# Attention tiles of a head pair ordered by query block first and head second, with the two heads' value products interleaved

## The reference

```python
sc = jnp.einsum('bhsd,bhmd->bhsm', q, mk).astype(jnp.float32) * (q.shape[-1] ** -0.5)
p = jax.nn.softmax(sc, axis=-1)
return jnp.einsum('bhsm,bhmd->bhsd', p.astype(mv.dtype), mv)
```

## Time and profile before

| what | value |
|---|---|
| median of 3 runs | 3445.1 us (3441.52 to 3446.01) |
| the profiled execution, its time | 3441.26 us |
| its span, first to last instruction | 3439.4 us |
| mean granted TensorE clock | 0.960 |
| PE busy | 3222.5 us, 94% of the span |
| DVE / ACT / POOL busy | 1401.9 / 745.3 / 1974.3 us |

### The profile page before, as it was taken

The page is one execution under the profiler, slowest core; times in us unless marked ns, Lnnn a source line. Parts: engine busy times, 40 slices in busy tenths (PEclk is TensorE's granted clock), DMA queues, the critical chain, the costliest instruction groups (busy, mean ns, idle before and its releaser), DMA issues.

```text
span 3439.4 us, 44451 instructions
## 1 busy us (share of the span) xinstructions
PE 3222.5 (94%) x14188; PEld 2516.5 (73%) x14188; DVE 1401.9 (41%) x2310; ACT 745.3 (22%) x1516; POOL 1974.3 (57%) x1528
## 2 busy tenths in 40 slices
PE   5898999999979889999999879989999999999998
PEld 3654887888756468788887656868888777878886
DVE  5545225221355352353425545452214544452223
ACT  3421102100234211120102335241002333230001
POOL 5234666776743266677767131847768433747765
PEclk8897999999989899999999889999999999999999
DMA  4111223222221122222222010322223111312222
GB/s 151 37 50 56 98 93 106 94 98 98 92 92 45 35 87 93 100 87 97 98 98 100 28 68 13 118 69 98 97 94 110 62 50 50 110 64 97 98 98 86
DMA packets 78347, 284.97 MB, mean 83 GB/s; under 512 B 8688, under 2 KB 9200, under 8 KB 77424
## 3 DMA queue, kind: packets, MB, share of 16 engines
q1 hardware_dynamic: 74736, 269.41, 23.1%
q10 hardware_dynamic: 3456, 13.50, 1.1%
HBM read 280.78 MB, written 2.10 MB: 82 GB/s over the span
## 4 chain that ended last, share of the span: by engine, by line
PE 78%; DVE 9%; ACT 3%; issue 1%; DVEq 0%; DMA 0%; ACTq 0%
PE pd L512 35%; PE pa L512 34%; PE pd L656 3%; PE po L675 3%; PE pa L664 1%; DVE b_lo L180 1%; DVE work L180 1%; DVE work L184 1%; ACT work L176 1%; DVE h_lo L188 1%; PE pd L575 1%; DVE pair L180 1%; DVE t L188 1%; PE pd L693 1%; PE po L707 1%
## 5 line engine op out<-in xcount | busy, mean ns | idle before, releaser
L465 POOL TENSOR_SCALAR w_hi<-w_raw 128x1024 fp32r<-128x1024 f32 x508 | 550.2, 1083 | 1392.9 <-PE pa L512 884.4
L512 PE MATMUL pa<-h_hi,w_hi 128*128 128x512 f32 x1888 | 754.1, 399 | 24.7 <-DVE h_lo L188 16.9
L469 POOL TENSOR_TENSOR w_lo<-w_raw,w_hi 128x512 fp32r<-128x512 f32 x508 | 743.5, 1464 | 0.0
L512 PE MATMUL pa<-h_lo,w_hi 128*128 128x512 f32 x1888 | 739.5, 392 | 0.0
L512 PE MATMUL pa<-h_hi,w_lo 128*128 128x512 f32 x1888 | 739.3, 392 | 0.0
L467 POOL TENSOR_TENSOR w_lo<-w_raw,w_hi 128x512 fp32r<-128x512 f32 x508 | 703.2, 1384 | 42.3
L512 PE MATMUL pd<-b_hi,w_hi 128*128 128x512 f32 x1152 | 456.8, 397 | 24.4 <-DVE b_lo L180 21.1
L512 PE MATMUL pd<-b_lo,w_hi 128*128 128x512 f32 x1152 | 452.4, 393 | 0.0
L512 PEld LDWEIGHTS pa<-h_hi,w_hi 128*128 128x128 f32 x1888 | 357.3, 189 | 129.8 <-issue 52.8
L512 PE MATMUL pd<-b_hi,w_lo 128*128 128x512 f32 x1152 | 451.7, 392 | 0.0
L512 PEld LDWEIGHTS pa<-h_lo,w_hi 128*128 128x128 f32 x1888 | 357.8, 190 | 75.9 <-issue 3.6
(11 more groups left out here) (154 smaller groups left out, 3417.9 us busy)
## 6 DMA issues: line engine op xcount, KB each, us to landing
w_raw<-in_w SPq DMA_DIRECT2D x508, 512.0 KB, 3.2
mrg<-in_mem ACTq DMA_DIRECT2D x4, 1024.0 KB, 4.8
mrg<-in_nabias ACTq DMA_DIRECT2D x2, 2048.0 KB, 8.7
x_res<-in_x SPq DMA_DIRECT2D x8, 256.0 KB, 5.7
out_y<-mrg ACTq DMA_DIRECT2D x8, 256.0 KB, 2.1
mrg<-in_count ACTq DMA_DIRECT2D x2, 512.0 KB, 3.9
kbuf<-in_delta ACTq DMA_DIRECT2D x2, 448.0 KB, 7.9
rope<-in_rope SPq DMA_DIRECT2D x1, 512.0 KB, 11.8
```

The costliest lines, as they stand in the source:

```text
L465: nc.gpsimd.tensor_scalar(w_hi[:, j], raw[:, j % RR], 1.0, 1.0, ALU.mult, ALU.mult).then_inc(rounded, 1)
L469: nc.gpsimd.tensor_tensor(w_lo[:, j, 512:1024], raw[:, j % RR, 512:1024], w_hi[:, j, 512:1024].bitcast(F32), ALU.subtract).then_inc(wsplit, 1)
L512: ins = mm(out, a, b, start=(first and k == 0 and e == 0), stop=(last and k == k_n - 1 and e == 2))
```

## The change

The list of tiles now has the query block outside and the head inside, so that the two tiles of a step are the two heads of one query block. Their scores are neighbours in PE's stream, from different halves of the rows and into different `pd` banks. The value products are collected until both tiles of the step are there (so both copies of `pt` are waited for ahead of the first product), and then issued alternately, head 0's first key block, head 1's first, head 0's second and so on; each tile's last product signals `pv_done`. For cross, with one head, the order of the products is unchanged, and only the two waits stand ahead of them. All engines follow the new list.

```diff
-        self.tiles = [(j, i) for j in range(self.heads) for i in range(ST)]
+        self.tiles = [(j, i) for i in range(ST) for j in range(self.heads)]
...
-                base = {}
+                base, two = {}, []
...
                         wait_read(pe, n, base[p, a])
-                        for k in range(kn):
-                            kt = NA_TILES[i][k] if ph.kind == "na" else k0 + k
-                            ins = mm(bank[ph.out_rows(j), P * i:P * i + P], ph.values(vbuf, p, j, kt),
-                                     pt[:, g % 2, k * P:k * P + P], start=(k == 0), stop=(k == kn - 1))
-                        ins.then_inc(pv_done, 1)
+                        kts = NA_TILES[i] if ph.kind == "na" else range(k0, k0 + kn)
+                        two.append([(bank[ph.out_rows(j), P * i:P * i + P], ph.values(vbuf, p, j, kt),
+                                     pt[:, g % 2, k * P:k * P + P], k) for k, kt in zip(range(kn), kts)])
+                        if a % 2 == 0:
+                            continue
+                        order = [x for both in zip(*two) for x in both] if ph.heads == 2 else two[0] + two[1]
+                        two.clear()
+                        for dst, val, prob, k in order:
+                            ins = mm(dst, val, prob, start=(k == 0), stop=(k == kn - 1))
+                            if k == kn - 1:
+                                ins.then_inc(pv_done, 1)
```

## The result

The changed kernel took 3423.95 us (median of four runs, 3419.4 to 3431.3) against 3444.55 in the same job (3441.5 to 3446.0): a ratio of 0.9943, interval 0.9922 to 0.9965. It is 20.6 us faster, a third of the 60 us forecast, and 6 us beyond the slow end of the range.

What follows compares the result with a forecast made beforehand. PE's stream was taken as the bound (busy 94%); 26 (dil) + 22 (mem, na) + 9 (swa) + 4 (mla) - 1 (cross) = 60 us gave 3385 us. Range: 8 in 10 between 3364 and 3418.

Steps and rivals of the forecast that it cites:

- drains at each change of the column half: Rival, value products: 0.15 us per change, 49 us, total 3464 or 3494; chance 0.06 together with any other loss.
- no overlap: Rival, scores and products: PE takes heads as it took tiles, only the order acts, 3445 within 3 us; chance 0.08.
- I take 11 us a layer, 22 us: Mem and na of both hybrid layers: 13.8 us a layer saved at full clock, less waits, leaves 22 us.
- It costs under 10 us, within the range: Rival, slow stretches of mem and swa: less busy PE stays at 1.2 GHz longer; under 10 us, no separate chance.
- I deducted 0.9 us where a wait follows directly: Mem and na: savings right before PE's waits for DVE only lengthen the wait, about 0.9 us each.
- dil, "26 us": Dil: 24.5 us for seven pairs with a successor and 1.5 for the last pair, 26 us gained.
- The 3.5 us a pair: Dil: 4.29 us saved of a pair's 31.5, 0.8 given back, 3.5 us gained for each pair with a successor.
- the bank wait: Dil, last step of a pair: the second score waits for the bank the rotation used, 0.8 us given back.
- The last pair ... I give it 1.5: Dil's last pair, without pieces, with DVE and ACT on its path: 1.5 us gained.
- swa, "9 us": Swa: 12 us for four pairs at full clock, three quarters taken because of waits after the rotation: 9 us gained.
- mla, "4 us": Mla: scores can't overlap, products could save 8.7 us, about half hidden by waits for DVE: 4 us gained.
- cross, "1 us lost": Cross: first of the last two tiles' products waits for both copies, about 0.5 us in each of two layers.

Runs made afterwards that it cites:

- early tails: Changed kernel, but in cross and each attention's last four tiles a head's products start with its own copy: 3415.35 us against 3447.06, ratio 0.9901.
- the control: Kernel before the change, with eleven unused matmuls in each na: 3444.83 us against 3445.63, ratio 1.0000.
- fillers are many: Unused matmuls in seven places of mem, na, swa, mla: on top of early tails 3415.46 us, in the kernel before 3450.98, both against 3446.9.
- na's fillers: Early tails plus seven and four unused matmuls in two places of na: 3405.52 us against 3450.12, ratio 0.9870.
- the order-only kernel: Changed kernel with products head by head and an 8-column full-array matmul between a step's two scores: 3475.99 us against 3447.06, ratio 1.0085.

## Why the prediction was wrong

**Right: the overlap and its prices.** Both kinds run two heads in one head's time, 0.63 and 0.59 us a step of two blocks against 0.64 and 0.59 forecast, and a pair of dil takes 28.35 us, inside the 27 to 30 that the prediction set as its test. One of the rivals, drains at each change of the column half, is excluded by the same rows, and "no overlap" too. On the same 128 rows sixteen records of two heads took 1.02 us, and eight of one head alone took 1.02 too. The Trainium skill's rule that a weight load overlaps matmuls in flight only when its row group differs ("TensorE: Matmul & The Clock Gate", Part 3, "The mechanism") does not hold for these products.

**The steps that failed: "I take 11 us a layer, 22 us" for mem and na, and "It costs under 10 us, within the range" for the clock.** Of the 39 us that are missing, the first term is the larger and the better measured: 4.1 us were lost in the windows, and nothing gained in the profile of the version with the products head by head, so about 22 are missing there. The prediction counted every step as work that PE bounds and deducted single waits, but the kernel before has 17.6 us of the second layer's na in its chain without a piece of PE (above).

The clock was named as a rival, placed in mem and swa, and left out of the sum. It fell in both halves of the hybrid layers' attentions, na most (141 to 208 us 0.97 before, 0.88 after), in the retention and pooling behind the second layer by 0.01, and in dil; in swa it is the same within 0.01. The granted clock of whole runs is 0.952 (median after) against 0.957 to 0.959 (medians of before in the later jobs). What a clock step is worth the single runs suggest: the five of the early tails run from 3406.93 us at 0.956 to 3419.89 at 0.951, 2.6 us for each thousandth, those of the control from 3439.38 at 0.961 to 3450.34 at 0.957, 2.7. Five to seven thousandths at 2.6 make 13 to 18 us, an estimate, and not under 10. This is a relation between runs of one kernel and not a measurement of the clock's price; between kernels it fails where fillers are many (0.006 more clock and no time, twice). What shows the cause are the two edits that take it away: early tails (9.9 us of waits, 8.5 us of time) and na's fillers (clock, 6 to 10 us). Together they bring back some 15 to 18 of the 39.

**The rest, term by term** (lengths from the windows, profiled executions, which differ by 10 us and not by 20.6).
- *mem and na, "22 us"*: -4.1, the wrong sign. I deducted 0.9 us where a wait follows directly, but PE saved 0.9 us in every step of a chain whose pace DVE sets at several places, and the wait for both copies (0.40 and 1.03 us) came on top. Then the clock fell from 0.91 to 0.83 and from 0.89 to 0.82.
- *What was not in the sum at all*: the unchanged work behind both attentions, 6.4 us longer, at 0.01 lower clock; 2.6 of it stands in the other profile too.
- *dil, "26 us"*: 15.1. The 3.5 us a pair were 3.15 (the bank wait 1.03, not 0.8), and the first chunk's clock took 2.7 once. "The last pair ... I give it 1.5" had the wrong sign: without pieces its path is DVE's and ACT's, and it took 20.9 us instead of 17.9. PE's timeline there after:

```profile
2892.11 1.96 PE L656 MATMUL pd<-kbuf,qbuf 64*128 64x512 f32 x4 [1.30 <-DVE nm L200]
...
2897.54 1.95 PE L664 MATMUL pa<-mats,work 128*128 128x128 f32 x8 [0.87 <-DVE work L184]
...
2902.45 1.09 PE L681 MATMUL po<-work,vbuf 128*64 128x128 f32 x16 [1.48 <-ACT work L176]
```

 The eight transposes take 1.95 us, 0.24 each, where they took 0.11; the clock is at 0.50 there.
- *swa, "9 us"*: 6.0; busy PE fell by 10.2 us and 4.2 became waiting. *mla, "4 us"*: 0.3; busy PE fell by 5.6 and 5.3 became waiting. *cross, "1 us lost"*: two waits of 0.6 us, 1.2.

**What stays open.** The split between clock and waits is not exact: a wait at the low clock counts in both. Some 20 us of the 39 came back by no edit. The single chunks don't follow a rule that I could read from the rows: the same chunk behind the same waits took 8.31 us in one version and 7.21 in another. And no run separates a clock lost to the waits from one lost because work of the same kind came to lie at another moment; in the order-only kernel the clock was as low as in the changed one.

## What to carry to other kernels

Before a change that only makes the busiest engine's work shorter, list its waits of a microsecond and more and the long run of matmuls behind each: what is saved ahead of them is given to the wait, and the matmuls behind may then run at 1.2 GHz, so the loss can exceed the gain. A busy share of 91% does not say that PE bounds a stretch; the chain that ended last does, if one reads it there. Where a step now needs two results, leave the last steps of a stage, which have no other work to hide the wait, as they were. A few unused matmuls inside a wait are worth a try only where they end before the wait does, and their gain has to be read from runs of one job, for single chunks can come out either way.

## What the hardware showed that I had not expected

Products into the two column halves overlap without being interleaved, for about four records (sixteen in 1.51 us, twelve in 1.07, where one head after the other would take 2.04 and 1.60). A full-array matmul of 8 columns between two half-array ones takes 0.20 us and makes each half pay its fixed 0.21 us again. Eleven matmuls a layer that compute nothing made a kernel of 3412 us 6.3 us faster in one job, and one with another order of the same work not at all (ratio 1.0000, 0.9992 to 1.0009).
